# Delta layer: the first half of one projection piece stands between the turns of the normalised queries and keys and the key products

## The reference, cut to what matters

```python
h = rmsnorm(x, g_pre) * (1.0 + scale) + shift
proj = h @ w_in                      # 3 x 512 columns of q, k, v; 512 of z; 4 + 4 of b and a
qkv = silu(causal_conv(qkv, conv_w))
q = l2norm(q) * 128 ** -0.5;  k = l2norm(k)
lmat = where(strict, einsum(k * beta, k) * decay, 0)
tmat = triangular_solve(lmat + eye, eye)
u = tmat @ (v * beta);  w = tmat @ (k * beta * exp(gc))
attn = einsum(q, k) * decay
# over the chunks, in order:
v_new = u_c - w_c @ S
o = qg_c @ S + attn_c @ v_new
S = S * gl_c + kg_c.T @ v_new
```

## Time and profile before

| what | us |
|---|---|
| median of 3 runs | 4112.31 |
| lowest and highest of them | 4110.48, 4113.34 |
| the profiled execution | 4110.52 |
| its span, first to last instruction | 4108.7 |
| TensorE busy with products | 3865.8 (94% of the span) |
| VectorE busy | 2650.0 (64%) |
| ScalarE busy | 1359.6 (33%) |
| GpSimd busy | 920.8 (22%) |
| granted TensorE clock, mean of the span | 0.981 of full speed |

### The profile page before, as it was taken

One profiled execution on the slowest core, in us unless ns is written; L12 is line 12 of the kernel. 1 busy time (PEld: TensorE's weight loads), 2 busy tenths in 40 slices (PEclk: granted clock), 3 DMA queues, 4 the chain that ended last, 5 costly groups with the idle time before them and its releaser, 6 DMA issues. The chain is left out here.

```text
span 4108.7 us, 59822 instructions
## 1 busy us (share of the span) xinstructions
PE 3865.8 (94%) x23331; PEld 2667.8 (65%) x23331; DVE 2650.0 (64%) x4968; ACT 1359.6 (33%) x2906; POOL 920.8 (22%) x543
## 2 busy tenths in 40 slices
PE   8999999998999999997999999998999999998877
PEld 5556555655666666656888888886665656665544
DVE  5666666655777777763566556653366777788875
ACT  1222222222211111112333333332354555655552
POOL 0344444433233322231222222221000000000000
PEclk9999999999999999999999999999999999999988
DMA  7343334333544434342000000012101000000000
GB/s 264 131 149 119 139 134 153 120 121 109 202 145 151 140 136 150 128 176 62 25 26 23 22 25 27 17 33 101 54 32 37 19 24 32 19 19 19 19 13 18
DMA packets 197087, 342.12 MB, mean 83 GB/s; under 512 B 20213, under 2 KB 100426, under 8 KB 196682
## 3 DMA queue, kind: packets, MB, share of 16 engines
q1 hardware_dynamic: 196810, 338.26, 23.4%
HBM read 298.90 MB, written 39.33 MB: 82 GB/s over the span
## 5 line engine op out<-in xcount | busy, mean ns | idle before, releaser
L249 PE MATMUL e_ps<-arena 128*128 128x386 f32 (+1 forms) x1960 | 653.6, 487 | 4.9 <-DMA arena<-l_w_in 2.4
L249 PEld LDWEIGHTS e_ps<-arena 128*128 128x128 f32 x1960 | 364.6, 191 | 249.4 <-issue 18.8
L249 PE MATMUL o_ps<-arena 128*128 128x320 f32 x1624 | 461.8, 436 | 18.7 <-DVE o_hh L321 5.2
L1726 PE MATMUL d_ps<-hT_in,arena 128*128 128x128 f32 x3072 | 393.6, 283 | 13.3 <-ACT hT_in L1945 11.3
L249 PEld LDWEIGHTS o_ps<-arena 128*128 128x128 f32 x1624 | 301.0, 191 | 147.5 <-issue 13.8
L1726 PEld LDWEIGHTS d_ps<-hT_in,arena 128*128 128x128 f32 x3072 | 360.7, 194 | 29.0 <-ACT hT_in L1945 12.6
L2766 PE MATMUL s_ps<-s_w_out,arena 128*128 128x512 f32 x512 | 257.1, 624 | 0.0
L2483 PE MATMUL s_ps<-hT_in,arena 128*128 128x128 f32 x2016 | 237.2, 277 | 0.0
L2483 PEld LDWEIGHTS s_ps<-hT_in,arena 128*128 128x128 f32 x2016 | 233.5, 194 | 2.4 <-issue 1.4
L3114 POOL TENSOR_TENSOR xb<-xb 128x1024 f32<-128x1024 f32 x16 | 37.6, 2351 | 879.7 <-DVE xb L3028 879.7
L3090 DVE SCALAR_TENSOR_TENSOR s_acc<-s_Lg,arena,s_acc 128x512 f32<-128x512 f32 (+3 forms) x266 | 171.0, 682 | 85.7 <-ACT s_Lg L2888 81.7
(11 more groups left out here) (522 smaller groups left out, 6892.0 us busy)
## 6 DMA issues: line engine op xcount, KB each, us to landing
arena<-l_w_in SPq DMA_DIRECT2D x48, 1024.0 KB, 7.7
arena<-l_w_in SPq DMA_DIRECT2D x32, 1040.0 KB, 8.3
xb<-x SPq DMA_DIRECT2D x64, 512.0 KB, 4.3
arena<-l_w_in SPq DMA_DIRECT2D x16, 1544.0 KB, 9.2
arena<-l_w_in SPq DMA_DIRECT2D x16, 1280.0 KB, 7.5
arena<-l_w_in SPq DMA_DIRECT2D x32, 504.0 KB, 6.9
arena<-l_w_in SPq DMA_DIRECT2D x16, 768.0 KB, 6.7
o_scratch<-w_ada SPq DMA_DIRECT2D x16, 768.0 KB
```

What stands on the lines that cost most here:

```text
L249: m = pe.matmul(bank[(g + k) % 2][:, 0:self.n], rows[:, kk * P:(kk + 1) * P], cols[:, kk, :], start=(kk == 0 and k in (0, 1, 4)), stop=(kk ...
L1726: m = pe.matmul(bank[c % 2][:, t * P:(t + 1) * P], W_in[:, k, (4 * c + t) * P:(4 * c + t + 1) * P], hT[:, k * P:(k + 1) * P], start=(k == ...
```

## The change

`project` takes a second argument that says which halves of a piece's products it issues. A new function `fill_half` issues the first half of the next piece and leaves the second half in the list; it is called once for a block, between `turn_normalised(j)` and `key_products(j)`. In the blocks 0 to 13 the piece is number 15, and its half is 2 of its 4 products. In the last two blocks it does nothing. The products, their operands and their number stay as they are, and so do the instructions of the other engines.

```diff
-            def project(i, n):
+            def project(i, n, halves=(0, 1)):
                 c, t = (n // 4, n % 4) if n < 12 else (3 + (n - 12) // 2, n % 2)
-                if t == 0:
+                if t == 0 and 0 in halves:
...
                 if c < 3:
-                    for k in range(KT):
+                    for k in range(4 * halves[0], 4 * halves[-1] + 4):
...
                 else:
                     a = QKV + (c - 3) * ZH
-                    for k in range(4 * t, 4 * t + 4):
+                    for k in range(4 * t + 2 * halves[0], 4 * t + 2 * halves[-1] + 2):
...
-                if t == (3 if c < 3 else 1):
+                if t == (3 if c < 3 else 1) and 1 in halves:
                     m.then_inc(*proj_made.inc())
...
+                def fill_half():
+                    if pieces and not b.last2:
+                        project(b.i + 2, pieces[0], (0,))
+                        pieces[0] = pieces[0], (1,)
+
                 def fill(n=1):
...
                         if not b.last2:
-                            project(b.i + 2, piece)
+                            project(b.i + 2, *(piece if isinstance(piece, tuple) else (piece,)))
...
                     turn_qk(j)
                     fill(3)
                     turn_normalised(j)
+                    fill_half()
                     key_products(j)
                 fill(17)
```

## The result

The changed kernel takes 4118.53 us (median of 20 runs, 4112.34 to 4122.98), the kernel before in its 20 runs 4111.69 us (4108.56 to 4113.34). The ratio is 1.0016, with a 95% interval of 1.0009 to 1.0023: slower by 6.8 us, clear of no change and a little less than the 8.2 us that the prediction called slower (it gave slower and no change 0.48 each). The prediction's 4122 us is 3.5 us above it.

A forecast was written before the change was run, and what follows sets the result against it. The prediction took TensorE to bound the layer, so time is won only where it stops waiting. Terms: +0.4 us cover and +10.5 us clock falls, +10.9 on 4110.5, giving 4121.4, taken as 4122 us; range 4111 to 4134.

The forecast's parts named there:

- The cover is exact to 0.03 us: Before the key products: the half piece fills the 0.78 us wait for kT; they start 0.03 us later, +0.4 us over 14.
- a full drain: Before the key products: they wait for the last record's end, as the skill's tiling-mode rule says; 14 x 0.1 = +1.4 us.
- What was filled in one wait is opened in the next, 1.03 to 1.91 us: Before the turns of T: TensorE's idle time grows by 0.88 us, as only 2 of piece 15's 4 products remain there.
- The clock falls behind the thinned stretch: Between key products and turns of T: work drops from 2.02 to 1.14 us, halving TensorE's clock in some blocks; chance 0.70.
- Rival (a): Delta layer: the clock holds and the change is no change, +0.4 us, 4111 to 4113 us; chance 0.20.
- (b): Before the key products: the cover doesn't hold, kT late or a longer wait; at most 12 us, likelier 4113 us; chance 0.06.
- (c): Turns of T: they wait only behind piece 15, not for T; up to 12 us faster, 4098 us; chance 0.04.
- 5 falls: Over the 14 changes of block: a share of 4 in 11 gives 5 clock falls, together +10.5 us.
- The share of 4 in 11: Earlier trace: of 11 full-clock stretches of 3.05 us with 0.94 to 1.30 us of work, 4 preceded a fall.
- 2.1 us a fall: Turns of T and of h: 1.3 us for the first stretch, plus a further stretch of 1.5 for every second fall.
- The 0.67 us of idle time doesn't absorb it, since it is the copy's time behind the turns: Wait for hT before the next projection's first piece: it takes up none of a fall's +1.64 us on the turns.
- The Trainium skill's rule that long gaps cost the clock: TensorE's idle gaps: they lower the clock only above a certain length, so 1.91 us is harmless; cited against the expected falls.

The follow-up runs named there:

- a filler: Changed kernel plus four 128 x 128 products of identity with ones, into an unread bank, behind piece 15's second half; 4110.06 us, ratio 1.0001 to the kernel before.
- the kernel with a wait of 0.19 us and a price of 1.27 us: Changed kernel with ScalarE's copies to hT moved ahead of the six softplus steps; 4115.08 us, ratio 1.0009 to the kernel before.

## Why the prediction was right, point by point

- *The cover is exact to 0.03 us.* Right. In the changed kernel the key products start 1.081 us behind the last turn, before 1.055. The row of block 0's preparation gave it; a full drain would have been 0.1 us.
- *What was filled in one wait is opened in the next, 1.03 to 1.91 us.* Right to the hundredth, and the key products to the turns of T still take 4.13 us.
- *The clock falls behind the thinned stretch.* Right, and it is the loss but for the 0.4 us of the cover: with a filler it is gone, with the first half left out it stays. Rival (a) is out; (b) and (c) would have moved the periods without a fall, which stayed at 57.62 us.
- *5 falls.* 7 in the 14 periods and an eighth at the head of block 14, in each of three traces. The share of 4 in 11 was a poor base: falls aren't independent draws. It was also miscounted: the trace of the kernel before has a twelfth such stretch, with 1.13 us of work, and the clock fell right behind it, so the share was 5 in 12.

```profile
1837.07:1840.12 3.05, 1.13 (x9) 0.70 (x7) 2.95 (x13) 1.10 (x3) 0.00 (x0) 1.00 1.06 395
1840.20:1843.50 3.30, 2.76 (x7) 1.73 (x8) 2.45 (x5) 0.98 (x3) 0.00 (x0) 0.50 1.06 399
```

- *2.1 us a fall.* This is the term that was mis-sized: 0.78 us, with periods of 58.4 us and not 59 to 61. Two steps of it failed. "The 0.67 us of idle time doesn't absorb it, since it is the copy's time behind the turns" was wrong: the first copy waited for ScalarE's softplus, and the wait took up 0.67 of 1.45 us, as the kernel with a wait of 0.19 us and a price of 1.27 us shows. And falls of 6.8 us were expected for every second; all in the 14 periods were of 3.4 us. 7 x 0.78 = 5.5 us stand where 5 x 2.1 = 10.5 were forecast: too few falls and too high a price partly cancelled, and that much of the closeness of 4122 us is luck.
- *The Trainium skill's rule that long gaps cost the clock* (TensorE: Matmul & The Clock Gate, "HAM oscillation") has gaps of 1.91 us harmless, and the traces disagree: within the 14 periods the clock fell at 7 of 13 of them, and at only 1 of 13 gaps of 2.34 us in the kernel with three products ahead; in block 14 of the kernel before it fell with gaps of 1.03 us at most.

Still open: of the 6.8 us between the medians the 14 periods account for 5.9. Block 14 took 1.3 us less than before in the first trace and 0.9 to 1.0 us more in the two others, so it may hold the rest; and as the interval of the ratio goes from 3.7 to 9.5 us, the rest needs no cause. Why the clock falls behind one thin stretch and not behind the next is open too.

## What to carry to other kernels

Moving work of the bounding engine from one wait into another gains nothing when both waits end on other engines' chains: what counts is whether the engine that they wait for is released earlier. Before a move out of a wait, ask what it leaves there: here a wait of 1 us beside 2 us of products was harmless, and nearly 2 us of waiting beside 1 us of products brought TensorE's clock down behind about every second such stretch. And before a wait is put down to the instruction that released it, look at what the releasing engine did just before: here six small activations stood ahead of the copy, and moving them was worth 7.9 us, more than any order of the products that was tried.

## What the runs showed of the hardware

- Behind a stretch of 3.05 us with 1.15 us of large products the clock fell to half in 7 of 13 cases within the 14 periods (8 of 13 with the first half left out, 10 of 13 with ScalarE's copies moved forward), and behind one with 1.58 us in none. With 1.15 us and, behind them, 1.15 us of 64 x 64 tiles, a quarter of the array each, it fell in none.
- Behind a stretch with only 0.7 us of products it fell in 1 of 13 cases where the periods were 58.05 us long, twice alike. Fewer falls don't mean a fuller stretch.
- A fall of 3.4 us slowed the products by 1.45 us, and lengthened the period by 0.78 or by 1.27 us, as a wait of 0.67 or of 0.19 us behind them took up the rest.
- The order of falls is repeatable: three traces of one kernel have them in the same 7 periods, and yet the times of its 20 runs are spread over 10.6 us, against 4.8 before.
